# Forget-gate mixer: two GLU channel tiles in token tiles ahead of the gate projection, the gate's log chain behind 17 convolution taps

## The reference, cut to what matters

```python
def odd_mixer(x, w_in, forget_b, dw_w, dw_b, cn_g, cn_b, w_out):
    p = x @ w_in                  # q | k | v (512 each) | forget gate (8) | GLU value, GLU gate (512 each)
    ...
    y_c = forgetting_attention(q, k, v, log_f)       # log_f = log_sigmoid(gate + forget_b)
    y_d = conformer_conv(p[..., 3 * D_C + H_C:], dw_w, dw_b, cn_g, cn_b)
    return jnp.concatenate([y_c, y_d], axis=-1) @ w_out

def forgetting_attention(q, k, v, log_f):
    cum = jnp.cumsum(log_f, axis=1)
    # logit[t,s] = q_t.k_s / 8 + cum[t] - cum[s], causal, softmax, times v

def conformer_conv(p_d, dw_w, dw_b, cn_g, cn_b):
    h = p_d[..., :D_D] * jax.nn.sigmoid(p_d[..., D_D:])     # GLU
    h = causal_dwconv(h, dw_w) + dw_b                       # 31 taps per channel
    return jax.nn.silu(layer_norm(h, cn_g, cn_b))
```

## Time and profile before

| | us |
|---|---|
| median of 3 runs | 2315.44 (2315.04 to 2315.79) |
| the profiled execution, its own time | 2316.31 |
| its span in the trace | 2314.5 |
| mean granted TensorE clock | 0.995 of full |

### The profile page before, as it was taken

The page is one execution under the profiler, slowest core; times in us unless marked ns, Lnnn a source line. Parts: engine busy times, 40 slices in busy tenths (PEclk is TensorE's granted clock), DMA queues, the critical chain, the costliest instruction groups (busy, mean ns, idle before and its releaser), DMA issues.

```text
span 2314.5 us, 24716 instructions
## 1 busy us (share of the span) xinstructions
PE 2267.8 (98%) x10295; PEld 1832.3 (79%) x10295; DVE 705.7 (30%) x1401; ACT 707.5 (31%) x1006; POOL 1027.0 (44%) x351
## 2 busy tenths in 40 slices
PE   7999999999999999999999999999999999999998
PEld 6667888888777778888888888888878667888887
DVE  7535000004377450000048420000159625000003
ACT  2443222222344323212222232222244573231220
POOL 3224554544333245545545655445442334454443
PEclk9999999999999999999999999999999999999999
DMA  4123332222222132222222333222222213222221
GB/s 172 65 83 109 110 107 93 91 85 79 91 74 85 43 127 92 91 99 93 100 89 99 109 109 102 98 91 89 77 91 90 76 43 131 101 97 91 101 82 55
DMA packets 33535, 214.72 MB, mean 93 GB/s; under 512 B 3720, under 2 KB 4872, under 8 KB 10000
## 3 DMA queue, kind: packets, MB, share of 16 engines
q1 hardware_dynamic: 32256, 211.03, 26.1%
q10 hardware_dynamic: 1168, 2.11, 0.3%
HBM read 211.02 MB, written 2.11 MB: 92 GB/s over the span
## 4 chain that ended last, share of the span: by engine, by line
PE 92%; DVE 4%; ACT 2%; POOL 1%; issue 1%; DMA 0%; SPq 0%; DVEq 0%; ACTq 0%
PE bank L989 17%; PE bank L991 17%; PE bank L990 17%; PE bank L1039 9%; PE bank L1041 9%; PE bank L1040 9%; PE bank L1175 2%; PE bank L1176 2%; PE bank L1180 2%; PE bank L1100 1%; PE bank L1218 1%; PE bank L1477 1%; PE bank L1451 1%; PE bank L1078 1%; POOL wlo L831 1%
## 5 line engine op out<-in xcount | busy, mean ns | idle before, releaser
L831 POOL TENSOR_TENSOR wlo<-raw,whi 128x2048 fp32r<-128x2048 f32 (+5 forms) x184 | 843.7, 4587 | 660.5 <-ACT whi L471 650.5
L989 PE MATMUL bank<-XH,whi 128*128 128x512 f32 x1736 | 685.3, 395 | 6.2 <-POOL wlo L887 6.2
L991 PE MATMUL bank<-XH,wlo 128*128 128x512 f32 x1736 | 677.9, 390 | 0.0
L990 PE MATMUL bank<-XL,whi 128*128 128x512 f32 x1736 | 677.3, 390 | 0.0
L471 ACT CAST whi<-raw 128x2048 fp32r<-128x2048 f32 (+5 forms) x184 | 349.3, 1900 | 380.7 <-PE bank L1039 304.5
L989 PEld LDWEIGHTS bank<-XH,whi 128*128 128x128 f32 x1736 | 326.8, 188 | 87.1 <-issue 14.0
L991 PEld LDWEIGHTS bank<-XH,wlo 128*128 128x128 f32 x1736 | 326.7, 188 | 68.8
L990 PEld LDWEIGHTS bank<-XL,whi 128*128 128x128 f32 x1736 | 327.2, 188 | 65.5
L1753 DVE TENSOR_TENSOR hf<-sil,bank 128x512 f32<-128x512 f32 x80 | 55.0, 688 | 814.5 <-PE bank L991 814.5
L1039 PE MATMUL bank<-whi,HH 128*128 128x512 f32 x704 | 274.6, 390 | 0.0
L1041 PE MATMUL bank<-wlo,HH 128*128 128x512 f32 x704 | 274.2, 389 | 0.0
(11 more groups left out here) (278 smaller groups left out, 2229.6 us busy)
## 6 DMA issues: line engine op xcount, KB each, us to landing
raw<-w_ffn_gu SPq DMA_DIRECT2D x88, 1024.0 KB, 4.8
raw<-w_ffn_dn SPq DMA_DIRECT2D x40, 1024.0 KB, 4.8
GB<-gb SPq DMA_DIRECT2D x8, 1024.0 KB, 6.8
raw<-w_diff_in SPq DMA_DIRECT2D x6, 1280.0 KB, 6.0
raw<-w_ev_in SPq DMA_DIRECT2D x6, 1024.0 KB, 4.9
raw<-w_od_in SPq DMA_DIRECT2D x4, 1536.0 KB, 6.3
raw<-w_mla_pair SPq DMA_DIRECT2D x4, 1088.0 KB, 5.5
raw<-w_mla_o SPq DMA_DIRECT2D x4, 1024.0 KB, 6.0
```

Of the source, the lines that this page charges most:

```text
L831: pool.tensor_tensor(wlo[:, off:off + size], raw[:, off:off + size], whi[:, off:off + size].bitcast(F32), ALU.subtract).then_inc(lo_ready, 1)
L989: release(pe.matmul(out, whi[:, off:off + P], xh, start=start, stop=False))
L990: pe.matmul(out, whi[:, off:off + P], xl, start=False, stop=False)
L991: return pe.matmul(out, wlo[:, off:off + P], xh, start=False, stop=stop)
```

## The change

It reorders the weights of the forget-gate mixer and its opening. The GLU channel tiles 0 and 1 are now two units in token tiles (`od_early`), done by `early_units` at the end of the third FFN (`ffn(True)`); `opening(2)` and the separate unit of GLU tile 1 go. ScalarE takes four sigmoids of 128x256, VectorE four products of 128x256 into `zt`, and TensorE brings `zt` back with 8 transposes behind the first 9 matmuls of the forget-gate unit, into banks 5 and 6. ScalarE copies tile 1 to `fz[1]` and the high part of tile 0 to `fzH`; VectorE, no longer GpSimd, makes `fzL`. ScalarE then writes diagonals 0 to 19 in one piece, and only after them splits the last GLU unit and starts the log chain. VectorE does 3 taps of tile 1 ahead of `lfz`, 14 behind it, then its part of the chain, and the other 14 taps behind that. The number of units is the same (13), one is placed by hand.

```diff
--- before.py
+++ after.py
@@ -77,11 +77,11 @@
 STREAM = [("mla_in", (3072, 3072)), ("mla_pair", (2176,) * 4), ("mla_o", OUT), ("ffn0", None),
           ("diff_v", (2048,) * 2), ("diff_qk", (2048,)), ("diff_in", (2560,) * 6 + (3072,)), ("diff_o", OUT), ("ffn1", None),
           ("ev_in", (2048,) * 6), ("ev_pool", (512,)), ("ev_b", (2048,) * 2), ("ev_o", OUT), ("ffn2", None),
-          ("od_glu0", (2048,)), ("od_f", (1024,)), ("od_glu", (2048,) * 3), ("od_in", (3072,) * 4), ("od_o", OUT),
+          ("od_early", (2048,) * 2), ("od_f", (1024,)), ("od_glu", (2048,) * 2), ("od_in", (3072,) * 4), ("od_o", OUT),
           ("ffn3", None)]
 
 
-PLACED = {("mla_o", 1): 4096, ("od_f", 0): 4096}
+PLACED = {("mla_o", 1): 4096, ("od_f", 0): 4096, ("od_glu", 1): 4096}
 
 
 def unit_table():
@@ -298,6 +298,10 @@
         lf_stack.close()
         fL = [[sb(f"fL{i}{m}", [P, S], F32, ph) for m in range(2)] for i in range(2)]
         fPT = [sb("fPT0", [P, NB, S], F32, ph), fPT1]
+        idle = ExitStack()
+        sgt = sb("sgt", [P, NB, 2 * P], F32, idle)
+        zt = sb("zt", [P, NB, 2 * P], F32, idle)
+        idle.close()
         fC = sb("fC", [P, 4, S], F32, ph)
         fYH = sb("fYH", [P, 2, S], F32R, ph)
         fQ = [sb(f"fQ{i}", [P, S], F32, ph) for i in range(2)]
...
@@ -678,23 +686,40 @@
             split_w(3)
             layer_norm((0, 1, 2, 3), True)
             ffn()
-            layer_norm((4, 5, 6, 7), False)
-
+            layer_norm((4, 5, 6, 7), True)
+
+
+            def diagonals(ks):
+
+                for k in ks:
+                    if k >= DIAGONALS:
+                        act.wait_ge(dg_used, k - DIAGONALS + 1)
+                    d = dg[k % DIAGONALS]
+                    act.activation(d[:, 0:P], ident, ACT.Copy, scale=cwH[:, k:k + 1].bitcast(F32))
+                    act.activation(d[:, P:2 * P], ident, ACT.Copy, scale=cwL[:, k:k + 1]).then_inc(dg_ready, 1)
 
             def sigmoid(i):
 
                 act.wait_ge(tile_done, tiles.at(2))
-                if i:
-                    act.wait_ge(tile_free, tiles.at())
+                act.wait_ge(tile_free, tiles.at())
                 act.activation(fsig[:], bank[GLU_BANKS[i][1]][:], ACT.Sigmoid).then_inc(gate_done, 1)
                 gates.add()
                 tiles.add(2)
 
-            split_w(2)
             act.copy(cwH[:], parm[:, PCOL["dw_w"]:PCOL["dw_w"] + 4 * TAPS:4]).then_inc(cw_hi, 1)
-            sigmoid(0)
-            act.wait_ge(tile_free, tiles.at())
-            act.copy(fzH[:], fz[0][:]).then_inc(act_hi, 1)
+            split_w()
+            for t in range(NB):
+                act.wait_ge(tile_done, tiles.at(t + 1))
+                act.activation(sgt[:, t, :], bank[t][:, 2 * P:4 * P], ACT.Sigmoid).then_inc(gate_done, 1)
+            gates.add(NB)
+            tiles.add(NB)
+            split_w()
+            act.wait_ge(gz_done, 1)
+            act.copy(fz[1][:, PADC:], bank[5][:]).then_inc(z_kept, 1)
+            act.wait_ge(gz_done, 2)
+            act.copy(fzH[:, PADC:], bank[6][:]).then_inc(z_high, 1)
+            act.wait_ge(cw_lo, 1)
+            diagonals(range(0, 20))
             split_w()
             tiles.add(1)
             act.wait_ge(tile_free, tiles.at())
@@ -707,16 +732,6 @@
             act.wait_ge(small_dve, 2)
             act.activation(lfl[:], lfu[:], ACT.Ln).then_inc(small_act, 1)
             small.add(2)
-            split_w()
-
-            def diagonals(ks):
-
-                for k in ks:
-                    if k >= DIAGONALS:
-                        act.wait_ge(dg_used, k - DIAGONALS + 1)
-                    d = dg[k % DIAGONALS]
-                    act.activation(d[:, 0:P], ident, ACT.Copy, scale=cwH[:, k:k + 1].bitcast(F32))
-                    act.activation(d[:, P:2 * P], ident, ACT.Copy, scale=cwL[:, k:k + 1]).then_inc(dg_ready, 1)
 
             def keep_conv(i, sem_, value):
 
@@ -743,17 +758,12 @@
                     h = 2 * p + m
                     act.dma_start(fB[p % 2][m][:], gate_rows[h:h + 1, :].to_broadcast([P, S])).then_inc(gate_in[p % 2], 16)
 
-            act.wait_ge(cw_lo, 1)
-            diagonals(range(0, 4))
-            sigmoid(1)
             act.wait_ge(cum_ready, 1)
             act.dma_start(gate_rows, cum[:]).then_inc(rows_out, 16)
-            diagonals(range(4, 16))
+            sigmoid(2)
+            diagonals(range(20, TAPS))
             act.wait_ge(rows_out, 16)
             gate_biases(0)
-            diagonals(range(16, 20))
-            sigmoid(2)
-            diagonals(range(20, TAPS))
             keep_conv(1, conv_done, 1)
             keep_conv(0, dg_used, TAPS)
             split_w()
@@ -924,9 +934,8 @@
             layer_norm()
             ffn()
             layer_norm()
-            split_w(2)
-            split_x(fzL[:], fz[0][:], fzH[:])
-            split_w(2)
+            pool.wait_ge(xn_ready, 2 * norms.n)
+            split_w(4)
 
             def diagonal_biases(p):
 
@@ -1528,7 +1537,7 @@
             for ks in OUT_KS:
                 out_steps(begin_unit(), ks, mixed)
             out_units(mixed)
-            ffn()
+            ffn(True)
 
 
             def conv_taps(ks):
@@ -1568,11 +1577,24 @@
                 value_end(ins, 6)
                 out_ready[p] = (va_free, vas.n)
 
-            opening(2)
-            unit_into((2,))
-            unit_into(GLU_BANKS[1])
-            pe.wait_ge(act_lo, los.at(1))
-            los.add()
+            def z_transposes():
+
+                for e, b in ((1, 5), (0, 6)):
+                    claim(b)
+                    for t in range(NB):
+                        ins = pe.transpose(bank[b][:, t * P:(t + 1) * P], zt[:, t, e * P:(e + 1) * P], ident)
+                    ins.then_inc(gz_done, 1)
+                freed[5], freed[6] = (z_kept, 1), (z_low, 1)
+
+            off, gated = begin_unit(), tiles.at()
+            claim(2)
+            for k in range(KD):
+                if k == 3:
+                    pe.wait_ge(tile_free, gated)
+                    z_transposes()
+                ins = product(bank[2][:], off + k * P, XH[:, k, :], XL[:, k, :], k == 0, k == KD - 1)
+            tile_end(ins, 2)
+            pe.wait_ge(z_low, 1)
             claim(7)
             conv_taps(range(0, 16))
             unit_into(GLU_BANKS[2])
@@ -2056,8 +2078,10 @@
             ffn()
 
 
-            for i in range(4):
-                dve.memset(fz[i][:, 0:PADC], 0.0)
+            for z in (fzH, fzL):
+                dve.memset(z[:, 0:PADC].bitcast(F32), 0.0)
+            for z in fz[1:]:
+                dve.memset(z[:, 0:PADC], 0.0)
 
             def glu(i):
                 dve.wait_ge(gate_done, gates.at(1))
@@ -2081,11 +2105,19 @@
                     else:
                         ins.then_inc(conv_done, 1)
 
-            glu(0)
             dve.wait_ge(cw_hi, 1)
             dve.tensor_tensor(cwL[:], parm[:, PCOL["dw_w"]:PCOL["dw_w"] + 4 * TAPS:4], cwH[:].bitcast(F32), ALU.subtract).then_inc(cw_lo, 1)
+            for t in range(NB):
+                dve.wait_ge(gate_done, gates.at(t + 1))
+                take(lambda: dve.tensor_tensor(zt[:, t, :], sgt[:, t, :], bank[t][:, 0:2 * P], ALU.mult))
+            gates.add(NB)
+            dve.wait_ge(z_high, 1)
+            dve.tensor_tensor(fzL[:, PADC:], bank[6][:], fzH[:, PADC:].bitcast(F32), ALU.subtract).then_inc(z_low, 1)
+            dve.wait_ge(z_kept, 1)
+            taps(3)
             take(lambda: dve.tensor_scalar(lfz[:], bank[2][0:8, :], parm[0:8, PCOL["f_b"]:PCOL["f_b"] + 1], None, ALU.add))
             link(dve.memset(lf0[:], 0.0))
+            taps(14)
             smalls.add(3)
             dve.wait_ge(small_act, smalls.at())
             dve.tensor_scalar(lfu[:], lfe[:], 1.0, None, ALU.add).then_inc(small_dve, 1)
@@ -2098,8 +2130,7 @@
             link(dve.scalar_tensor_tensor(lfz[:], lfz[:], -1.0 / HD_SCALE, lfc[:], ALU.mult, ALU.add))
             dve.tensor_tensor_scan(cum[:], lfz[:], lf0[:], 0.0, ALU.add, ALU.add).then_inc(cum_ready, 1)
 
-            glu(1)
-            taps(TAPS)
+            taps(TAPS - 17)
             glu(2)
             taps(TAPS)
             glu(3)
...
@@ -2226,7 +2257,9 @@
     win = f(inp["od_w_in_2"])[0]
     w["od_f"] = unit(win[:, 1536:1664])[None]
     glu = win[:, 1544:2568].reshape(KD, P, 2, 4, P).transpose(3, 1, 0, 2, 4).reshape(4, P, 2048)
-    w["od_glu0"], w["od_glu"] = glu[0:1], glu[1:]
+    early = np.concatenate([win[:, 1544:1544 + 2 * P], win[:, 2056:2056 + 2 * P]], 1)
+    w["od_early"] = early.reshape(2, 4, P, HALF).transpose(0, 2, 1, 3).reshape(2, P, 2048)
+    w["od_glu"] = glu[2:]
     w["od_in"] = win[:, 0:1536].reshape(KD, P, 3, 4, P)[:, :, vqk].transpose(3, 1, 0, 2, 4).reshape(4, P, 3072)
     m = f(inp["od_w_out_2"])[0].reshape(KD, P, D)
     w["od_o"] = down(np.concatenate([m[k] for k in ODD_SETS[0] + ODD_SETS[1]]), (4, 4))
```

More of the change, by code:

```diff
@@ L382, in build @@
         rope_ready = sem("rope_ready")
+        gz_done = sem("gz_done")
+        z_kept = sem("z_kept")
```

(4 more changed lines are left out.)

## The result

Twenty runs of each kernel gave medians of 2320.06 us for the changed kernel (2318.09 to 2323.83) and 2316.61 us for the one before (2315.04 to 2317.83): a ratio of 1.0017, 95% interval 1.0011 to 1.0024. That is 3.45 us more and within the 0.2% that the prediction calls no change; the interval, whose upper end is 0.24%, leaves no doubt that it is a small loss. The forecast was + 4.2 us. That its 2319.6 lies only 0.46 us off is partly luck: it stood on the median of three runs, 1.17 us lower than that of twenty.

A forecast was written before the change was run, and what follows sets the result against it. TensorE, busy 2267.8 of 2314.5 us, was taken to bound the kernel. A loop start 2.6 us later plus 1.6 us of clock gave + 4.2, so 2320.5, or 2319.6 as median (+ 0.18%); range 2314.8 to 2323.0.

The forecast's parts named there:

- The entry: Forget-gate mixer's opening on TensorE: priced from the gated-conv mixer, the convolution starts at 1728.08, 4.20 us earlier.
- VectorE's path: VectorE from tile 1's taps to the copy of K: held to decide, the loop starts 2.6 us later.
- the hold: VectorE's lfu and the chain behind it: GpSimd's low half on the shared port pair costs 1.3 us more.
- The cause of the idle time: VectorE ahead of lfu: 4.0 us idle, as ScalarE's diagonal 19 waits for tap 15, then the cast and chain follow.
- TensorE's lead: TensorE, convolution to loop: loses 1.4 us for diagonal 20, perhaps 0.6 for a low half, then waits 5 to 6.
- The clock: TensorE's half clock behind its wait at the loop's start: 1.6 us lost, bounds 0 and 5.2.
- rival B: Loop's first step: half clock through most of it, up to 5.2 us, so up to 2323.2, slower; chance 0.34.
- passes on undiminished: Scan loop: the shift of K's copy reaches the end in full, as the loop's order, taps and units are untouched.
- C: Before the loop: ScalarE's exponential comes during the 14 taps, TensorE's lead survives, 2312.7, at best 2311.2; chance 0.10.
- D: ScalarE's log chain: two dearer table switches, 1.3 us each, make K's copy 2.6 us later, 2322.2; chance 0.02.
- A: Loop's start slips, the time stays within 4.6 us: 2316.7 to 2320.0, the forecast itself; chance 0.54.

The follow-up runs named there:

- e3: Changed kernel with ScalarE's cast of the last GLU unit moved behind its log chain: 2317.59 us, 1.0004 of the kernel before.
- e8: Changed kernel with six diagonal buffers instead of four and the cast of the last GLU unit behind the log chain: 2316.06 us, 0.9998 of before.
- e6: Changed kernel with six diagonal buffers instead of four: 2319.95 us, 1.0017 of the kernel before.
- e2: Changed kernel with 22 unused matmuls filling TensorE's wait at the loop's start: 2318.07 us, 1.0009 of the kernel before.
- e9: e5 with four unused matmuls ahead of TensorE's wait in the loop's fifth step: 2311.64 us, 0.9980 of the kernel before.
- e1: Changed kernel with 21 instead of 14 VectorE taps ahead of its part of the log chain: 2313.43 us, 0.9988 of the kernel before.
- e5: e1 with GLU tile 2's sigmoid and two diagonals ahead of the wait for cum, one tap moved behind K's copy: 2312.34 us, 0.9984 of before.
- e7: Changed kernel with GLU unit 2 ahead of the convolution and nine unused matmuls at the loop's start: 2313.90 us, 0.9990 of the kernel before.

## Why the prediction was right, step by step

Predicted (from the reference point) against measured:

| step | predicted at + | measured at + |
|---|---|---|
| convolution starts on TensorE | 29.81 | 29.91 |
| VectorE's 14 taps end | 42.98 | 42.76 |
| `lfu` starts | 47.03 | 47.00 |
| scan ends | 52.93 | 52.84 |
| tile 1's taps end (the next product starts) | 63.93 | 63.69 |
| copy of K starts | 96.63 | 96.38 |

**The entry** was priced from the gated-conv mixer's rows, and came out within 0.1 us. Taking the price from a place in the same trace where the same form already ran included the clock and the waits without having to name them.

**VectorE's path** decided, as forecast: idle 4.0 predicted, 4.24 measured; the hold 1.3 and 1.31. For the hold, rows 9 had shown a VectorE operation ending 0.29 us behind the low half; here it was 0.28, and e3 showed it gone. It agrees with the Trainium skill's rule (SBUF — State Buffer, who interferes with whom), by which one of the two engines holds the shared port pair for a whole instruction. Something from the other side fits it too: in e3 and e8 the low half begins beside VectorE's scan, and takes 5.28 us instead of 4.61.

**The cause of the idle time was only half named.** The prediction said that diagonal 19 waits for tap 15, and then comes the cast. True as far as it goes, but e6 shows that the cast would have waited for the next matmul anyway. The two cannot be told apart in the trace, as the later one in ScalarE's list finds its wait already over.

**TensorE's lead**: the wait for diagonal 20 was 1.10 us (1.4 predicted), and there was no 0.6 us for the q, k, v low half. TensorE ended that unit at + 91.22 (+ 91.7 predicted) and stood 5.91 us (5 to 6).

**The clock** is the term that was mis-sized: 1.6 predicted, 2.30 measured. The prediction took two waits of about 3 us as the nearest rows, and overlooked a nearer one in the same trace, a wait of 4.66 us (TensorE in before: timeline, then windows):

```profile
55.93 0.76 PE L989 MATMUL bank<-CH,whi 128*128 128x512 f32 x1 [4.66 <-DVE mKN L1665]
```

```profile
55.90:63.00 7.10, 7.07 (x22) 5.68 (x23) 4.37 (x7) 0.03 (x1) 4.83 (x1) 0.68 0.17 38
```

Behind it 7.10 us ran at 0.68 of full clock, which is an estimated 2.3 us lost (7.10 x 0.32). As the term's price that would have met the 2.30; but the same wait in the changed kernel's trace is followed by 7.10 us at 0.79, 1.5 us lost, so a row of this kind gives a range and not a value. The 2.30 us alone are past the 2.0 us from which rival B was to decide. It did not, for two reasons. The fifth step gave back 0.95 us, which the prediction did not know of, though the half clock of that step stands in the trace of before (0.66 from 1818 to 1823). The fourteenth step took 0.82 us. The prediction's sentence that the shift "passes on undiminished" was wrong by these two, which nearly cancel, and the loop's start was 0.24 us better than forecast. That they cancel is luck, and so is part of the total's agreement.

**The rivals.** C fell, as the exponential came 4.24 us too late. D fell: VectorE goes on 2.03 us behind the start of the exponential's table load (1743.60 - 1741.57), exactly as in rows 7 and 8. The Trainium skill (ScalarE: Activation LUTs, What ACT_TABLE_LOAD costs) has 2.66 us for a switch with its drain; here the load takes 1.28 us and the exponential starts 1.30 us behind the load's start, and the measurement decides. B's mechanism is real, at under half its upper price. The median of 2320.06 us lies just above A's own 2316.7 to 2320.0, which stood on a base 1.17 us too low; counted from the kernel before, its 3.45 us are A's.

**What stays open.** Why a given wait lowers the clock in one trace and not in another isn't settled: the same 2.38 us at step fourteen left it at 1.00 before and cost 0.82 us after, and the same 4.66 us near the start cost 2.3 us in one trace and 1.5 in the other. A filler for the wait at step fourteen was not tried. The medians differ by 3.45 us, which lies between the spans' 2.9 and the 4.57 that the changed stretch shows; single runs of the changed kernel spread over 5.7 us, and the longest of them have the lowest mean clock (0.995 in the run of 2318.09 us, 0.993 in that of 2323.83), so a trace is one draw, and the sum of its terms is known better than how often each of the clock's is drawn.

## What to carry to other kernels

A chain that is moved into another engine's work has to be placed by when its input comes, not by how much work there is: seven taps on the wrong side of the chain moved the loop's start by 5.06 us, more than the 4.10 us that the whole new opening gave TensorE. When a wait goes away and another stays, ask what else hangs on the same event; here two waits of ScalarE ended with two matmuls in a row, and six buffers gave 0.29 us alone (e6) but 1.37 us once the cast was out of the way (e3 to e8). And where the engine that bounds the kernel has to wait, count the clock behind the wait as a term of its own, and look for the other stretches at half clock in the trace of before: they may leave or come back.

## What the runs showed of the hardware

**Half clock wanders.** In every kernel but e2 and e9 the loop had one costly stretch at half clock in its first five steps, in step one or in step five, never in both: where step one had 5.13 or 5.14 us, step five had 8.37 to 8.40 (before, e1, e5, e7); where step one had 6.75 to 7.90, step five had 7.45 to 7.47. The two waits of step five (0.96 to 1.02 us, and 0.74) were nearly the same either way. e2 and e9 had neither; e2's fillers stood ahead of step one, as did those of e7, whose step five was not spared. Each kernel has one trace, so how often this holds is not shown.

**The price doesn't follow the length of the wait.** Waits of 2.39, 2.88, 4.24, 5.88 and 5.91 us cost 1.61, 2.76, 2.19, 2.56 and 2.30 us of first step. The shortest is the cheapest, but the dearest is the next shortest.

**Useless matmuls can pay**: in the traces 4 of them shortened a step by 0.93 us (e9) and 22 by 2.32 us (e2), each step then at the length that it has at full clock. 9 of them won 1.62 us in one step, and 0.90 were lost again four steps later (e7). Between the medians these gains are 0.7, 2.0 and 0.4 us, none of them beyond the intervals.
